# Delta layer: when the second weight pair is loaded and summed in a look-ahead Strassen-Winograd projection

## The reference, cut to what matters

```python
u = jnp.dot(hmod, w_in)
qkv, z, b, a = jnp.split(u, ODD_SPLITS, axis=-1)
qkv_c, new_buf = causal_dwconv(qkv, conv_buf, conv_w)
...
t_mat = unit_lower_inverse(a_mat, cb)
...
v_new = u_i - jnp.einsum('bhck,bhkv->bhcv', w_i, state)
o_i = (jnp.einsum('bhck,bhkv->bhcv', q_i * jnp.exp(g_i)[..., None], state)
       + jnp.einsum('bhcj,bhjv->bhcv', qk_i, v_new))
...
state = state * jnp.exp(g_last)[..., None] + jnp.einsum('bhck,bhcv->bhkv', k_dec, v_new)
```

## Time and profile before

| | |
|---|---|
| median of 3 executions | 1416.29 us (1416.02 to 1417.29) |
| the profiled execution, its own time | 1415.07 us |
| span of its instructions | 1413.3 us |
| TensorE busy | 1364.9 us, 97%, 12976 matmuls |
| VectorE busy | 822.2 us, 58% |
| ScalarE busy | 439.0 us, 31% |
| GpSimd busy | 269.5 us, 19% |
| granted TensorE clock | 0.999 of full speed |
| one head that looks ahead | about 89 us, heads 0 to 6 from about 618 to 1241 us |

### The profile page before, as it was taken

The page is one execution under the profiler, slowest core; times in us unless marked ns, Lnnn a source line. Parts: engine busy times, 40 slices in busy tenths (PEclk is TensorE's granted clock), DMA queues, the critical chain, the costliest instruction groups (busy, mean ns, idle before and its releaser), DMA issues.

```text
span 1413.3 us, 30732 instructions
## 1 busy us (share of the span) xinstructions
PE 1364.9 (97%) x12976; PEld 929.3 (66%) x12976; DVE 822.2 (58%) x1834; ACT 439.0 (31%) x1062; POOL 269.5 (19%) x402
## 2 busy tenths in 40 slices
PE   5999999999999999999999999999999999989998
PEld 3577765666653445667777777778777778765543
DVE  4747772444432344775866858668486685862244
ACT  4114441444420322522323323233232331422211
POOL 1113200000000111431412314123141231310111
PEclk9999999999999999999999999999999999999999
DMA  9520108000055301201103022030120300430133
GB/s 367 227 48 32 38 0 326 1 1 1 3 226 226 129 30 60 59 32 34 62 3 95 34 56 73 3 94 35 30 98 3 95 34 6 164 136 25 47 119 119
DMA packets 56317, 112.16 MB, mean 79 GB/s; under 512 B 34698, under 2 KB 37586, under 8 KB 53346
## 3 DMA queue, kind: packets, MB, share of 16 engines
q1 hardware_dynamic: 56180, 110.21, 22.4%
HBM read 91.79 MB, written 18.40 MB: 78 GB/s over the span
## 4 chain that ended last, share of the span: by engine, by line
PE 65%; DVE 4%; issue 2%; ACT 0%; DVEq 0%; POOLq 0%; POOL 0%; ACTq 0%
PE psum L929 62%; PE psum L932 2%; DVE mem L2533 1%; DVE mem L2513 0%; DVE mem L2422 0%; DVE mem L2574 0%; DVE mem L2758 0%; DVE mem L2753 0%; DVE mem L2768 0%; DVE mem L2756 0%; DVE mem L2624 0%; DVE mem L2737 0%; DVE mem L2419 0%; DVE mem L2776 0%; DVE mem L2854 0%
## 5 line engine op out<-in xcount | busy, mean ns | idle before, releaser
L929 PE MATMUL psum<-mem 32*32 32x32 f32 (+11 forms) x12368 | 1304.1, 290 | 27.7 <-issue 10.0
L929 PEld LDWEIGHTS psum<-mem 32*32 32x32 f32 (+5 forms) x12368 | 860.4, 137 | 436.4 <-issue 231.1
L2533 DVE SCALAR_TENSOR_TENSOR mem<-mem 128x576 f32<-128x576 f32 (+1 forms) x126 | 112.3, 891 | 0.0
L932 PE MATMUL psum<-mem 128*128 128x128 f32 (+1 forms) x608 | 85.9, 278 | 15.0 <-ACT mem L1619 10.8
L932 PEld LDWEIGHTS psum<-mem 128*128 128x128 f32 (+1 forms) x608 | 71.3, 144 | 41.1 <-issue 25.7
L760 POOL TENSOR_SCALAR mem<-mem 128x1 f32<-128x1 f32 x17 | 3.6, 212 | 343.8 <-ACT mem L1762 343.8
L1926 ACT ACTIVATE mem<-mem 128x128 f32<-128x128 f32 x72 | 22.0, 305 | 135.3 <-DVE mem L2776 82.1
L2375 DVE SCALAR_TENSOR_TENSOR mem<-psum,mem 128x1024 f32<-128x1024 f32 x12 | 15.2, 1271 | 60.4 <-POOL mem L762 60.4
L1741 ACT ACTIVATE mem<-mem 128x256 f32<-128x256 f32 x72 | 35.5, 494 | 46.4 <-DVE mem L2335 46.4
L1762 ACT ACTIVATE mem<-psum 128x1024 f32<-128x1024 f32 x12 | 12.3, 1024 | 110.5 <-PE psum L929 108.7
L2075 DVE TENSOR_SCALAR mem<-psum,mem 128x128 f32<-128x128 f32 x64 | 21.1, 404 | 39.1 <-PE psum L932 39.1
(11 more groups left out here) (242 smaller groups left out, 1191.4 us busy)
## 6 DMA issues: line engine op xcount, KB each, us to landing
mem<-modw SPq DMA_DIRECT2D x12, 2048.0 KB, 13.3
mem<-w SPq DMA_DIRECT2D x44, 512.0 KB, 4.3
mem<-x SPq DMA_DIRECT2D x1, 4608.0 KB, 18.1
x_dram<-mem SPq DMA_DIRECT2D x9, 512.0 KB, 2.6
mem<-row_dram SPq DMA_DIRECT2D x8, 576.0 KB, 6.3
mem<-x_dram SPq DMA_DIRECT2D x9, 512.0 KB, 3.7
mem<-wout SPq DMA_DIRECT2D x4, 1024.0 KB, 8.6
mem<-gs SPq DMA_DIRECT2D x8, 512.0 KB, 3.3
```

The lines of the kernel that those rows point to most:

```text
L929: return pe.matmul(*a, **k)
L932: return pe.transpose(out, in_, ident[0:n, 0:n])
L2533: x = dve.scalar_tensor_tensor(cvm, U1[:, m, lo + j:hi + j], CW[:, 3 * g + ORDER[m], j:j + 1], cvm, ALU.mult, ALU.add)
```

## The change

Two moves, both only in heads that look ahead. SyncE loads the second pair's buffers for head h+1 ahead of the wait for the scan's first state, when `n_ev1` has reached 7h+4; the waits that free the buffers stay with them. GpSimd makes the second pair's three sums at the end of `rest`, after the inverse's copies, and no longer as the first thing of `scan`. What is computed is the same, and so are TensorE's, VectorE's and ScalarE's programs.

```diff
@@ SyncE, head(h, ahead)
+                if ahead:
+                    sp.wait_ge(sem("n_ev1"), 7 * h + 4)
+                    if h:
+                        sp.wait_ge(sem("st_mm"), passed(h, 1, "3"))
+                        weights(h + 1, 2)
+                    else:
+                        sp.wait_ge(sem("pj_mm"), 12)
+                    weights(h + 1, 3)
                 sp.wait_ge(sem("st_ready"), 8 * h + 1)
...
                 if ahead:
                     sp.wait_ge(sem("s1_ready"), 3 * h + 3)
                     history(h + 1)
-                    if h:
-                        sp.wait_ge(sem("st_mm"), passed(h, 1, "3"))
-                        weights(h + 1, 2)
-                    else:
-                        sp.wait_ge(sem("pj_mm"), 12)
-                    weights(h + 1, 3)
                     sp.wait_ge(sem("eq_ready"), 3 * h + 3)
@@ GpSimd, end of rest(h, ahead)
                 c.tell(i, sem("diag_ready"), 2 * h + 2)
                 c.sync()
+                if ahead:
+                    head_sums(h + 1, 1)
@@ GpSimd, scan(h, ahead)
                 if ahead:
-                    head_sums(h + 1, 1)
                     hist1(h + 1, 0)
```

## The result

| | before | after |
|---|---|---|
| median | 1416.15 us (4 runs beside the changed kernel, 1415.62 to 1417.29) | 1407.47 us (4 runs, 1403.66 to 1407.95) |
| ratio, 95% interval | | 0.9931, 0.9918 to 0.9943 |
| the profiled execution / its span | 1415.07 / 1413.3 us | 1403.66 / 1401.9 us |
| TensorE busy | 1364.9 us, 97% | 1360.5 us, 97% |
| VectorE busy | 822.2 us, 58% | 809.7 us, 58% |

Faster by 0.69%, that is 9.8 us (8.1 to 11.6) by the ratio and 8.7 us between the two medians, where 8.5 us were forecast. The profiled execution of the changed kernel is the fastest of its four (the others took 1407.41 to 1407.95), so the difference of the two spans, 11.4 us, is more than the change is worth.

A forecast was written before the change was run, and what follows sets the result against it. Bound by TensorE's matmul stream (97% busy), so only closing its gaps pays. 9.2 us recovered less 0.7 for loads beside the dense stretch gives 8.5 us faster: 1416.29 to 1407.8 us, range 1406.0 to 1412.0.

The forecast's parts named there:

- part 5: Loads beside TensorE's dense stretch (730 to 738 us) slow its instruction blocks: 0.1 us a head, 0.7 us; bounds 0 and 5.3.
- Three sums leave the scan: Second pair's sums leave the scan in seven heads, closing TensorE's gaps: 9.2 us recovered, 6.2 if only visible gaps count.
- part 3: GpSimd's queue: new wait of some 2 us for step 7 holds up only the history copies behind the sums; cost 0.
- Part 1: TensorE gaps in seven heads: 6.2 us visible plus hidden time, 9.2 us recovered, 7.8 without the assumed part.
- the 0.20 us: Hidden time per gap: derived for L2737 from head 1 against head 0, assumed for each of seven L2768 gaps.
- Part 2: Sums at the inverse's end, near 741.6 to 745.7 us, lengthen no VectorE operation; price 0.
- Part 4: SyncE's loads wait for the fourth inverse update, issue near 731.6, land near 737.6 us; nothing behind is delayed; cost 0.
- The 0.38 us: Possible lengthening by loads of a gap with no engine behind it: 1.44 us in head 7 against 1.06 in head 5.
- A: Rival: the L2737 gap stays in the scan, so only 5.7 us faster, 1410.6 us; chance 0.10.
- B: Rival: sums start after 755 us and still lengthen VectorE's operations, or other small work fills the room: 1416.3 us; chance 0.08.
- C: Rival: instruction blocks starve behind the loads, TensorE stands 2.0 us in each of seven heads, slower, 1421.1 us; chance 0.04.

The follow-up runs named there:

- the kernel held to chunk 2: Changed kernel, loads early, but GpSimd waits for the new values of the scan's chunk 2 before the three sums: 1417.86 us, ratio 1.0014.
- the first group: The first four experiments in running order, measured with their own runs of the kernel before, median 1416.19 us.

## Why the prediction was right, and where it was wrong

**The whole.** 1407.8 us forecast, 1407.47 measured, by the mechanism that was named: the sums met VectorE's operations on two SBUF operands, and TensorE waited for what stood behind these. That the two times agree to 0.3 us is in part luck: the gaps were worth 1.0 us more than forecast, the 0.7 us taken off for part 5 are shown by no run, and the four executions of the changed kernel lie from 1403.66 to 1407.95 us.

**The step that was wrong** is the reading of the change as two moves, "Three sums leave the scan" by a move in GpSimd's program. In GpSimd's queue they did not move by one instruction; only SyncE's loads did. The prediction had both facts (the sums began when the weights had landed; `scan` follows `rest`) and costed the move at nothing in part 3, which came out right, without seeing why: it is nothing. So part 3's new wait of some 2 us for step 7 is not new in program order either; before, it had long been met when the sums came to it.

**Part 1, the sum of the gaps.** 9.2 us forecast, 10.2 measured in the stretches. Visible gaps were 6.2 us as read; hidden time was 4.0 and not 3.0. In head 1 two visible gaps of 0.77 us were 1.30 us of time. Where it lies shows when the start of each matmul, counted from the landmark ahead of the scan, is set against that of the same matmul in the changed kernel. In head 1 the stream is on time up to the L2768 gap, 0.67 us late behind it (0.41 visible) and 1.31 us late behind the L2737 gap (0.36 more visible). So 0.27 us were hidden under either, and heads 3 to 6 have the same. The mis-sized term is thus the 0.20 us, and not only where it was assumed: the five L2737 gaps gave back 3.2 us where 2.8 were counted, the seven L2768 gaps 6.3 where 5.6 were, the L2753 gaps the 0.8 counted. The 0.20 came out too small because head 0, taken as the control, lost another 0.07 us itself behind its gap.

**Part 2, the new place.** Free as said: sums at 1.26 us each, no lengthening, and six operations fit too. They started with step 7's second half as forecast: 739.03 against 741.6, where the landmark ahead of the scan (734.51 against 737.26) is itself 2.75 us earlier. The rule of the Trainium skill, "SBUF — State Buffer", section "Who interferes with whom", agrees on both sides with the kernel held to chunk 2: with two SBUF operands L2762 went from 0.42 to 1.43 us, with one L2772 stayed at 0.34.

**Part 4, SyncE's queue.** "Nobody waited for them" was true of the row broadcast before, and too short as a reason: nobody waited because the sums made VectorE late. With small sums and late loads the broadcast ended the wait in two of seven heads, and cost 1.0 us in that execution. The change is spared that, since its loads left first. The loads were issued at 728.88, with the end of the fourth update (728.40 + 0.45), as said.

**Part 5, instruction blocks.** 0.7 us taken. Between the stretches both profiled spans have 295.0 us, so a cost shows nowhere; but one kernel's instructions gave 295.0 and 297.0 in two executions, so 0.7 can't be told from 0. The 0.38 us from which it was taken is no price of loads either: over the fourteen traces the gap at head 5's place, without loads, was 0.80 to 1.42 us and that at head 7's 0.60 to 3.32, 2.71 of them before the four loads went out. In the window that the prediction named the loads do stand (DMA share 0.40 against 0.02 in the earlier trace rows), and TensorE was busy for all of it:

```profile
728.00:736.00 8.00, 8.00 (x166) 6.32 (x155) 5.00 (x10) 0.56 (x2) 1.69 (x5) 1.00 0.40 136
```

**The rivals.** A (the L2737 gap stays) fell: no gap, as head 0 had shown. B (the sums still meet VectorE) is what the kernel held to chunk 2 does, at its named time: 1417.86 for 1416.3. Its point, a start less than 4 us ahead of that operation (755 against 759.05), is consistent with the runs: harmless 5.1 us ahead, at full price 0.1 us ahead. Gaps such as C named come with the loads 12 us earlier and not at the change's place; they were 0.24, 1.08 and 1.51 us in heads 0 to 2 and nothing in the others, against 2.0 worked out for each of seven.

## What to carry to other kernels

Before costing a moved call, lay the two programs of its engine side by side, instruction by instruction: a call that moves from the end of one function to the start of the next has not moved, and the wait inside it (here for a DMA) sets its time. Where one operation is lengthened by another engine, what waits behind it is covered too: before calling a transfer "waited for by nobody", ask if that would hold without the delay. Two landmarks in the bound engine's stream, and the time between them, tell a change of 0.1 us where the median can't tell 2.

## What the runs showed that was not expected

The stretches between landmarks repeat head by head to 0.02 us across the changed kernel and ten of the experiments (45.94 to 46.00), while the rest of the same span (the time between stretches) varies between 295 and 304 us. Executions of one kernel spread over up to 7 us (those of the kernel before over 5.5 to 7.0 in each group), roughly with the mean granted clock: the kernel before in the first group had a median of 1415.4 us in seven runs at 0.998, 1417.3 in six at 0.997, and its slowest run, 1419.21 us, was at 0.994. As far as one profiled execution of each kernel shows, all of the change's gain is in the part that repeats, and the noise in the part that does not. One piece of that noise can be named: in nine of the twelve experiments' traces the granted clock stood at its lower level for some microseconds in head 7, in eight behind the gap at the head's start (2.2 to 3.3 us long there), in one behind the two later waits shown above. In the traces of before and of the change, with a gap of 1.44 us, it did not fall. Nor did it behind such gaps of 2.50 and 2.75 us in two others, so the length of a gap alone does not decide. And the gaps without a releaser in dense runs of 32-wide matmuls are not fixed: at one place in head 7 the same instructions had 1.44 us in one execution and 3.32 in another. What they are no run here settles; that loads issued just ahead of such a run can bring new ones is shown (in three heads of seven), that they are fetches of instructions is only argued.
